# One stage for the four heads of a recurrent (mLSTM) layer, with the next head's products placed between the units of a head's recurrence

## The chip, the core and the metric

The kernel runs on one core of a Trainium2 chip. The metric is the device time of one execution in microseconds (us), median of the runs. A change of 0.3% is about 11 us here.

## The reference, cut to what matters

A four-layer network on 1024 tokens of width 1024. The change touches one mixer of it, the chunkwise mLSTM with 4 heads of width 192, chunks of 128 tokens, run once forward and once backward (`q` and `k` come from a convolved input, `k` with the factor 192 ** -0.5):

```
    def step(carry, inp):
        C, n, m = carry
        ...
        dexp = jnp.exp(d - m_t[..., None])
        iexp = jnp.exp(inter - m_t)
        s = jnp.einsum('bhtd,bhsd->bhts', qb, kb) * dexp
        num = jnp.einsum('bhts,bhse->bhte', s, vb) + iexp[..., None] * jnp.einsum('bhtd,bhde->bhte', qb, C)
        den = jnp.sum(s, axis=-1) + iexp * jnp.einsum('bhtd,bhd->bht', qb, n)
        h = num / jnp.maximum(jnp.abs(den), jnp.exp(-m_t))[..., None]
        ...
        C_new = cexp[..., None, None] * C + jnp.einsum('bhs,bhsd,bhse->bhde', wexp, kb, vb)
```

## The kernel before, in words

The program is a row of stages. Each stage is a block with its own semaphores: every engine runs its own instruction list, written out by hand in program order, and a barrier of all engines ends the stage. TensorE (PE) writes to eight PSUM banks, VectorE (DVE) and ScalarE (ACT) empty them. All matmuls of this part are in fp32; in the trace one such matmul is two MATMUL records.

`ml_layer` works the heads one after the other, with two stages for each, eight in all:

- `products` (L2025): PE makes qT and kT of the head (8 jobs of two matmuls of 512 columns, L2037), then its keys with the tokens on the partitions (8 jobs of two matmuls of 192 columns). The jobs go round all eight banks. DVE empties the even jobs (L158, L159), ACT the odd ones (L156).
- `recurrence` (L2296): PE spreads the gate sums over partitions (16 matmuls of 128 columns, L2325, into four banks, "spread") and makes q times k of each chunk (16 matmuls of 128 columns, L2332, "raw"). DVE zeroes the state (L2390) and adds a mask to each spread bank (L2394). ACT copies raw out of PSUM (L2365) and takes 16 exponentials (L2371), 8 for each direction. DVE multiplies exponentials and raw, one instruction for each direction (L2399), and that gives the weights of the two directions.
- Then come 16 units, in turn forward and backward. In a unit PE makes one matmul with the weights ("intra", L2345), two matmuls that update the state, from the keys scaled by ACT (L2351, kw L2378; not in the last two units), and two with the state ("inter", L2358). Each of these five has 193 columns. ACT scales inter into `carried` (L2385). DVE makes the new state (L2409), adds carried and intra to `num` (L2417), makes the denominator in three short instructions (L2421 to L2423) and writes the head's output (L2426 or L2430). PE may begin intra of unit u when num of unit u-2 is there.

After the fourth head comes the stage `head_norm` (L2435), which begins with DVE on `hs`.

## Time and profile before

| what | us |
|---|---|
| median of 3 runs (3794.08, 3789.55, 3781.88) | 3789.55 |
| the profiled execution, its own time | 3775.88 |
| its span in the profile | 3774.2 |
| PE busy in the span | 3372.5 (89%) |
| DVE busy | 1926.9 (51%) |
| ACT busy | 1375.9 (36%) |
| mean granted TensorE clock | 0.934 |

The profile is one execution. Its own time lies 13.67 us below the median of the three runs. A row of the timeline has the start and the duration, then engine, line, operation, output and inputs; in brackets stands how long the engine sat idle before it and who released it. A MATMUL's end is modelled. In a row of a list of stretches each engine has its busy us and its number of records. PEclk is the granted clock: 1.00 is 2.4 GHz, 0.50 is 1.2 GHz, and a figure between is a stretch that holds both.

### The profile page before, as it was taken

The numbers are of one execution on the slowest core, as the hardware profiler recorded it, in microseconds if no ns is written. First come the engines' busy times: TensorE is split into PE (matmuls) and PEld (weight loads), VectorE is DVE, ScalarE is ACT, GpSimd is POOL, SyncE is SP. The second block draws the span as 40 slices with busy tenths as digits, with TensorE's granted clock in tenths as the row PEclk, the third lists the DMA queues.
The fourth block names the chain that finished last, engine by engine and source line by source line (L and its number), as shares of the span: only waits on it lengthen the run. The fifth ranks groups of instructions, "written<-read, shape, count | busy, mean of one in ns | idle before, by whom it ended". The sixth has DMA issues, their size and how long they took to land. (4 is left out here: it accounts for less than half of the span.)

```text
span 3774.2 us, 51016 instructions
## 1 busy us (share of the span) xinstructions
PE 3372.5 (89%) x19671; PEld 2663.6 (71%) x19671; DVE 1926.9 (51%) x3394; ACT 1375.9 (36%) x2544; POOL 359.7 (10%) x295
## 2 busy tenths in 40 slices
PE   7999988799989978849789998799889999998899
PEld 6884466688857766647478887589755678885557
DVE  4526645657646735474647655623255442325554
ACT  2006641556642132233146555501254420114442
POOL 0100000223330000000023323100100000001000
PEclk9999999799999988869889999899889999988999
DMA  6517023678865200012258867511000221110003
GB/s 204 182 42 227 1 101 112 223 279 331 334 260 175 93 20 1 1 56 79 112 189 323 327 219 264 199 34 42 16 1 1 96 90 34 33 25 1 1 15 131
DMA packets 250408, 459.85 MB, mean 122 GB/s; under 512 B 45043, under 2 KB 118087, under 8 KB 249801
## 3 DMA queue, kind: packets, MB, share of 16 engines
q1 hardware_dynamic: 231753, 389.70, 29.3%
q0 software_dynamic: 18432, 67.12, 4.7%
q8 instruction: 148, 2.42, 0.3%
q14 instruction: 75, 0.61, 0.0%
HBM read 380.72 MB, written 73.33 MB: 120 GB/s over the span
## 5 line engine op out<-in xcount | busy, mean ns | idle before, releaser
L1727 PE MATMUL psum<-high_in,e_rowsT_high 128*128 128x256 f32 (+1 forms) x1080 | 330.1, 324 | 5.4 <-DVE e_rowsT_low L174 5.4
L1728 PE MATMUL psum<-high_in,e_rowsT_low 128*128 128x256 f32 (+1 forms) x1080 | 326.2, 320 | 0.0
L174 POOL TENSOR_TENSOR low_down<-w_down,high_out 128x1024 fp32r<-128x1024 f32 x64 | 192.6, 3026 | 326.0 <-ACT high_out L1801 326.0
L1727 PEld LDWEIGHTS psum<-high_in,e_rowsT_high 128*128 128x128 f32 x1080 | 206.6, 191 | 22.4 <-issue 6.1
L1728 PEld LDWEIGHTS psum<-high_in,e_rowsT_low 128*128 128x128 f32 x1080 | 206.9, 192 | 16.2
L3457 DVE TENSOR_REDUCE mla_low<-psum 128x1 f32<-128x256 f32 (+7 forms) x128 | 91.0, 753 | 151.6 <-PE psum L3323 151.6
L174 DVE TENSOR_TENSOR low_gate<-w_gate,high_in 128x1024 fp32r<-128x1024 f32 x128 | 147.9, 1218 | 0.1
L174 DVE TENSOR_TENSOR low_up<-w_up,high_in 128x1024 fp32r<-128x1024 f32 x128 | 148.0, 1218 | 0.0
L279 PE MATMUL psum<-ring_high,s_x_high 128*128 128x512 f32 (+3 forms) x768 | 135.4, 319 | 5.6 <-DVE ring_high L169 5.6
L283 PE MATMUL psum<-ring_low,s_x_high 128*128 128x512 f32 (+3 forms) x768 | 136.7, 321 | 2.9 <-DVE ring_low L174 2.9
L285 PE MATMUL psum<-ring_high,s_x_low 128*128 128x512 f32 (+3 forms) x768 | 134.8, 318 | 0.0
L1801 ACT ACTIVATE high_out<-w_down 128x1024 fp32r<-128x1024 f32 x128 | 124.8, 1050 | 23.8 <-DMA w_down<-in_exp_w_down 23.8
L1732 PE MATMUL psum<-low_up,e_rowsT_high 128*128 128x256 f32 x720 | 130.3, 283 | 0.0
L158 DVE COPY proj<-psum 128x512 f32<-128x512 f32 (+2 forms) x40 | 20.6, 514 | 212.8 <-PE psum L285 212.8
L279 PEld LDWEIGHTS psum<-ring_high,s_x_high 128*128 128x128 f32 x768 | 113.9, 191 | 16.5 <-issue 6.0
L156 ACT ACTIVATE proj<-psum 128x512 f32<-128x512 f32 (+2 forms) x40 | 18.3, 457 | 293.4 <-PE psum L285 293.4
L1801 ACT ACTIVATE high_in<-w_gate 128x1024 fp32r<-128x1024 f32 x128 | 124.8, 1058 | 0.0
L1801 ACT ACTIVATE high_in<-w_up 128x1024 fp32r<-128x1024 f32 x128 | 124.7, 1054 | 0.0
L283 PEld LDWEIGHTS psum<-ring_low,s_x_high 128*128 128x128 f32 x768 | 114.3, 192 | 14.5 <-DVE ring_low L174 4.0
L1856 POOL COPY e_index<-moe_ids 128x1 uint32 (+1 forms) x49 | 9.6, 195 | 1189.0 <-POOLq L84 563.8
L285 PEld LDWEIGHTS psum<-ring_high,s_x_low 128*128 128x128 f32 x768 | 113.9, 191 | 10.5
L156 ACT ACTIVATE mla_probsT<-psum 128x512 f32<-128x512 f32 (+2 forms) x96 | 52.2, 544 | 180.4 <-PE psum L3338 180.4
(592 smaller groups left out, 7945.9 us busy)
## 6 DMA issues: line engine op xcount, KB each, us to landing
w_gate<-in_exp_w_gate SPq DMA_DIRECT2D x32, 2048.0 KB, 10.3
w_up<-in_exp_w_up SPq DMA_DIRECT2D x32, 2048.0 KB, 15.3
w_down<-in_exp_w_down SPq DMA_DIRECT2D x32, 2048.0 KB, 21.9
ada<-in_ada_w SPq DMA_DIRECT2D x24, 1024.0 KB, 6.8
expert_rows<-e_out POOLq DMA_DIRECT2D x47, 512.0 KB, 7.0
expert_rows<-zero_row SPq DMA_DIRECT2D x33, 512.0 KB, 6.9
token_rows<-x SPq DMA_DIRECT2D x32, 512.0 KB, 2.6
x<-token_rows SPq DMA_DIRECT2D x24, 512.0 KB, 6.9
```

The lines of the kernel that those rows point to most:

```text
L156: return eng.activation(dst, src, ACT.Copy, scale=1.0 if scale is None else scale)
L158: return eng.tensor_copy(dst, src)
L174: return eng.tensor_tensor(low, whole, high, ALU.subtract)
L279: pe.matmul(dst, lhsT, rhs, start=(m == 0), stop=False)
L283: pe.matmul(dst, lhsT, rhs, start=False, stop=False)
L285: mm = pe.matmul(dst, lhsT, rhs, start=False, stop=(m == len(ops) - 1))
L1727: pe.matmul(dst, rows_high[:, k, :], w_high[:, k, cols], start=(k == 0), stop=False)
L1728: pe.matmul(dst, rows_low[:, k, :], w_high[:, k, cols], start=False, stop=False)
L1732: mm = pe.matmul(dst, rows_high[:, k, :], w_low[:, k, cols], start=False, stop=(k == KT - 1))
L1801: act.activation(high(e, j)[:, k:k + STEP[j], :], W[e % 2][j][:, k:k + STEP[j], :], ACT.Copy).then_inc(s["w_high_ready"], 1)
L1856: pool.tensor_copy(index[:, :], ids[:, bass.ds(i, 1)]).then_inc(s["index_ready"], 1)
L3457: dve.tensor_reduce(low[:, n, side:side + 1], scores_of(n, side), AX.X, ALU.min).then_inc(s["lows_ready"], 1)
```

## The change

`products` and `recurrence` go, and `heads` takes their place: one stage for all four heads. The work that prepares a head is cut into 18 items (`HeadItems`): 8 qk items (two matmuls of 512 columns each), 4 keys items (two token tiles, four matmuls of 192 columns, in one bank), 4 spread items (four of 128) and 2 raw items (eight of 128). Head 0's items run first, then its exponentials. In each unit of heads 0 to 2, PE makes one or two items of the next head behind its inter; units 14 and 15 have none. Items have two banks, 4 and 5, in turn, and an item waits until the item two before it is emptied. ACT now empties all qk, keys and raw items, behind `carried` of the same unit, and takes the next head's exponentials after units 12 and 13. DVE masks the next head's spreads after units 8 to 11 and makes its weights after units 14 and 15. qT, keys and decay have two buffers each, kT and raw one. The first two units of a head lose inter and carried (the state is zero there): the state and num are plain copies, and the zeroing of the state goes. The math is otherwise as before.

```diff
--- before.py
+++ after.py
@@ -1984,25 +1984,7 @@
-    for h in range(ML_HEADS):
...
-        products(nc, core, jobs)
-        recurrence(nc, core, h, qT, kT, keys, vals, table, hs)
+    heads(nc, core, xcT, wq, vals, table, hs)
...
+class HeadItems:
...
+        self.order = [("qk", j) for j in range(8)]
+        for m in range(4):
+            self.order += [("keys", m), ("spread", m)]
+        self.order += [("raw", 0), ("raw", 1)]
+        self.per_head = {"qk": 8, "keys": 4, "spread": 4, "raw": 2}
+        self.steps = [[("qk", u)] for u in range(8)] + [[("keys", m), ("spread", m)] for m in range(4)] + [[("raw", 0)], [("raw", 1)], [], []]
...
+    qT = [m.at("ml_qT", W + at * KB, [HF, 2, SEQ]) for at in (32, 96)]
+    kT = m.at("ml_kT", W + 40 * KB, [HF, 2, SEQ])
+    keys = [m.at("ml_k", at, [P, TILES, ML_DH]) for at in (AT_XT + 25 * KB, W + 112 * KB)]
+    decay = [m.at("r_decay", W + at * KB, [P, DIRS, TILES, P]) for at in (18, 104)]
...
+    def item_bank(kind, i):
+        return bank[4 + items.at(kind, i) % 2]
...
+            def prepare(H, kind, i):
+                earlier = items.two_earlier(kind, H, i)
+                if earlier:
+                    pe.wait_ge(emptied[earlier[0]], earlier[1])
+                dst = item_bank(kind, i)
+                if kind == "qk":
+                    a, n, cols, _ = qk_of(H, i)
+                    for j, f in pieces_of(H):
+                        mm = pe.matmul(dst[0:HF, :], wq.of(a, H, j)[:, n * HF:(n + 1) * HF], xcT[:, f, cols], start=(j == 0), stop=(j == 1))
+                    mm.then_inc(s["qk_ready"], 1)
...
+            for kind, i in items.order:
+                prepare(0, kind, i)
+            for h in range(ML_HEADS):
+                for u in range(U):
+                    n, d, chunk, j = unit(h, u)
+                    q = slice(chunk * P, (chunk + 1) * P)
+                    if u < DIRS:
+                        pe.wait_ge(s["probs_ready"], DIRS * h + u + 1)
+                    if U * h + u >= 2:
+                        pe.wait_ge(s["num_ready"], U * h + u - 1)
+                    pe.matmul(bank[u % 2][:, 0:DV], decay[h % 2][:, d, chunk, :], vals[:, chunk, h, :], start=True, stop=True).then_inc(s["intra_ready"], 1)
+                    if u < V:
+                        at = V * h + u
+                        pe.wait_ge(s["kw_ready"], at + 1)
+                        if at >= 2:
+                            pe.wait_ge(s["state_ready"], at - 1)
+                        for k in range(2):
+                            mm = pe.matmul(bank[6 + u % 2][0:HF, k * 256:k * 256 + DV], kw[:, at % 3, k * HF:(k + 1) * HF], vals[:, chunk, h, :],
+                                           start=True, stop=True)
+                        mm.then_inc(s["update_ready"], 1)
+                    if u >= DIRS:
+                        at = V * h + u - DIRS
+                        pe.wait_ge(s["state_ready"], at + 1)
+                        if at >= 2:
+                            pe.wait_ge(s["carried_ready"], at - 1)
+                        for k in range(2):
+                            mm = pe.matmul(bank[2 + u % 2][:, 0:DV], qT[h % 2][:, k, q], state[:, d, n % 2, k, :], start=(k == 0), stop=(k == 1))
+                        mm.then_inc(s["inter_ready"], 1)
+                    if h + 1 < ML_HEADS:
+                        for kind, i in items.steps[u]:
+                            prepare(h + 1, kind, i)
...
+                if kind == "raw":
+                    act.wait_ge(s["raw_ready"], items.count("raw", H, i))
+                    if H:
+                        act.wait_ge(s["probs_ready"], DIRS * H)
+                    act.activation(raw[:, 4 * i:4 * i + 4, :].rearrange("p c q -> p (c q)"), src, ACT.Copy).then_inc(s["raw_copied"], 1)
...
+            for kind, i in items.order:
+                copy_item(0, kind, i)
+            for d in range(DIRS):
+                exponents(0, d)
+            for h in range(ML_HEADS):
+                act.wait_ge(s["keys_copied"], 4 * h + 4)
+                for i in range(U + 1):
...
+                    if u >= DIRS:
+                        n, d, chunk, j = unit(h, u)
+                        act.wait_ge(s["inter_ready"], V * h + u - DIRS + 1)
+                        act.wait_ge(s["num_ready"], U * h + u - 1)
+                        act.activation(carried[:, u % 2, :], bank[2 + u % 2][:, 0:DV], ACT.Copy,
+                                       scale=E[:, IEXP * S + j:IEXP * S + j + 1]).then_inc(s["carried_ready"], 1)
+                    if u >= 0 and h + 1 < ML_HEADS:
+                        for kind, k in items.steps[u]:
+                            copy_item(h + 1, kind, k)
+                        if u in (12, 13):
+                            exponents(h + 1, u - 12)
...
+                        if u < DIRS:
+                            if h:
+                                dve.wait_ge(s["inter_ready"], V * h)
+                            dve.tensor_copy(state[:, d, 1, :, :], update).then_inc(s["state_ready"], 1)
...
+                    if u >= DIRS:
+                        dve.wait_ge(s["carried_ready"], V * h + u - DIRS + 1)
+                        dve.tensor_tensor(num[:, u % 2, :], carried[:, u % 2, :], bank[u % 2][:, 0:DV], ALU.add).then_inc(s["num_ready"], 1)
+                    else:
+                        dve.tensor_copy(num[:, u % 2, :], bank[u % 2][:, 0:DV]).then_inc(s["num_ready"], 1)
...
+                    if h + 1 < ML_HEADS:
+                        if 8 <= u < 12:
+                            mask(h + 1, u - 8)
+                        if u >= 14:
+                            weigh(h + 1, u - 14)
```

The order on PE around the end of head 0. Before (L2345 intra, L2351 update, L2358 inter, L2037 products, L2325 spread, L2332 raw; L81 is a stage's end):

```order
L2345 MATMUL psum<-ml_v_14671,r_decay_15158 128x193
L2358 MATMUL psum<-r_state_15160,ml_qT_15046 128x193 x2
L81 UNCONDITIONAL_BRANCH
L2030 UNCONDITIONAL_BRANCH
L2037 MATMUL psum<-ml_xcT_13226,ml_wqkv_14672 96x512 x16
L2037 MATMUL psum<-ml_wqkv_14672,ml_xcT_13226 128x192 x16
L81 UNCONDITIONAL_BRANCH
L2320 UNCONDITIONAL_BRANCH
L2325 MATMUL psum<-neg_uT_14692,consts_49 128x128 x16
L2332 MATMUL psum<-ml_qT_15755,ml_kT_15756 128x128 x16
L2345 MATMUL psum<-ml_v_14671,r_decay_15867 128x193
```

With the change, from unit 13 of head 0 to unit 0 of head 1 (L2358 intra, L2365 update, L2374 inter, L2345 raw, L2326 qk; decay 15051 is head 0's, 15052 head 1's):

```order
L2358 MATMUL psum<-ml_v_14671,r_decay_15051 128x193
L2365 MATMUL psum<-ml_v_14671,r_kw_15055 96x193 x2
L2374 MATMUL psum<-r_state_15054,ml_qT_15046 128x193 x2
L2345 MATMUL psum<-ml_qT_15047,ml_kT_15048 128x128 x8
L2358 MATMUL psum<-ml_v_14671,r_decay_15051 128x193
L2374 MATMUL psum<-r_state_15054,ml_qT_15046 128x193 x2
L2358 MATMUL psum<-ml_v_14671,r_decay_15051 128x193
L2374 MATMUL psum<-r_state_15054,ml_qT_15046 128x193 x2
L2358 MATMUL psum<-ml_v_14671,r_decay_15052 128x193
L2365 MATMUL psum<-ml_v_14671,r_kw_15055 96x193 x2
L2326 MATMUL psum<-ml_xcT_13226,ml_wqkv_14672 96x512 x2
```

The 64 matmuls that stood between two heads are spread over the units; six matmuls of 193 columns (units 14 and 15) now stand between the last raw item and the next head's first intra.

ACT at the same place with the change (L2418 kw, L2425 carried, L2396 raw copy, L2403 exponential), from the end of unit 12 on:

```order
L2425 ACTIVATE r_carried_15056<-psum,exps_14690 128x193
L2396 ACTIVATE r_raw_15053<-psum 128x512
L2403 ACTIVATE r_decay_15052<-r_decay_15052,a_14682 128x128 x8
L2425 ACTIVATE r_carried_15056<-psum,exps_14690 128x193
L2396 ACTIVATE r_raw_15053<-psum 128x512
L2403 ACTIVATE r_decay_15052<-r_decay_15052,a_14682 128x128 x8
L2425 ACTIVATE r_carried_15056<-psum,exps_14690 128x193 x2
L2418 ACTIVATE r_kw_15055<-ml_k_15050,exps_14690 128x192
```

Carried of units 13 and 14 now stands behind a raw copy and 8 exponentials each; before, `carried` alternated with kw alone. On DVE the next head's first weights stand between the last two units:

```order
L2489 SCALAR_TENSOR_TENSOR ml_hs_14673<-r_num_15057,r_den_15058,ml_hs_14673 128x192
L2444 TENSOR_TENSOR r_decay_15052<-r_decay_15052,r_raw_15053 128x1024
L2474 TENSOR_TENSOR r_num_15057<-r_carried_15056,psum 128x193
L2480 SCALAR_TENSOR_TENSOR r_den_15058<-r_num_15057 128x1
L2481 TENSOR_SCALAR r_den_15058<-r_den_15058,exps_14690 128x1
L2482 RECIPROCAL r_den_15058<-r_den_15058 128x1
L2489 SCALAR_TENSOR_TENSOR ml_hs_14673<-r_num_15057,r_den_15058,ml_hs_14673 128x192
L2444 TENSOR_TENSOR r_decay_15052<-r_decay_15052,r_raw_15053 128x1024
L2461 COPY r_state_15054<-psum 96x386
```

So the first weights (the first L2444) wait for the output of unit 14 of the head before, and the second for that of unit 15.

## Rows read from the trace of the kernel before

**Rows 1.** The page's first line, and the stretch of the four heads (engines' busy us, clock)

```profile
span 3774.2 us, 51016 instructions
...
1363.00:1641.00 278.00, 238.24 (x1120) 182.89 (x1120) 147.49 (x436) 84.45 (x225) 0.00 (x0) 0.89 0.00 1
```

**Rows 2.** Timeline, head 0 from its first product to its first unit

```profile
1363.87 15.64 PE L2037 MATMUL psum<-ml_xcT,ml_wqkv 128*96 128x512 f32 x32 [2.94 <-PEq L84]
...
1379.35 5.36 PE L2037 MATMUL psum<-ml_wqkv,ml_xcT 128*128 128x192 f32 x32
...
1385.79 3.81 PE L2325 MATMUL psum<-neg_uT,consts 64*128 64x128 f32 x32 [1.08 <-PEq L84]
...
1389.53 3.84 PE L2332 MATMUL psum<-ml_qT,ml_kT 96*128 96x128 f32 x32
...
1393.40 0.60 ACT L2365 ACTIVATE r_raw<-psum 128x512 f32<-128x512 f32 x1 [1.19 <-PE psum L2332]
1393.90 4.77 ACT L2371 ACTIVATE r_decay<-r_decay,a 128x128 f32<-128x128 f32 x16
1396.44 1.22 DVE L2399 TENSOR_TENSOR r_decay<-r_decay,r_raw 128x1024 f32<-128x1024 f32 x1 [6.11 <-ACT r_decay L2371]
...
1397.81 0.98 PE L2345 MATMUL psum<-ml_v,r_decay 128*128 128x193 f32 x2 [4.44 <-DVE r_decay L2399]
...
1402.52 0.36 DVE L2417 TENSOR_TENSOR r_num<-r_carried,psum 128x193 f32<-128x193 f32 x1 [1.12 <-ACT r_carried L2385]
```

**Rows 3.** Timeline, end of head 0 and start of head 1's products

```profile
1427.85 0.35 DVE L2417 TENSOR_TENSOR r_num<-r_carried,psum 128x193 f32<-128x193 f32 x1
...
1429.20 0.35 DVE L2417 TENSOR_TENSOR r_num<-r_carried,psum 128x193 f32<-128x193 f32 x1
...
1431.46 16.59 PE L2037 MATMUL psum<-ml_xcT,ml_wqkv 128*96 128x512 f32 x32 [3.32 <-PEq L84]
```

**Rows 4.** Timeline, first unit of head 3 and last instruction of the fourth recurrence

```profile
1606.57 0.98 PE L2345 MATMUL psum<-ml_v,r_decay 128*128 128x193 f32 x2 [4.44 <-DVE r_decay L2399]
...
1640.23 0.42 DVE L2430 SCALAR_TENSOR_TENSOR ml_hs<-r_num,r_den,ml_hs 128x192 f32<-128x192 f32 x1
```

**Rows 5.** Timeline, copies of every second 512-column product in head 0

```profile
1370.97 0.69 DVE L158 COPY ml_qT<-psum 96x512 f32<-96x512 f32 x1 [3.90 <-PE psum L2037]
...
1374.40 0.69 DVE L159 TENSOR_SCALAR ml_kT<-psum 96x512 f32<-96x512 f32 x1 [2.75 <-PE psum L2037]
```

**Rows 6.** Timeline, intra of two early units and num of two late units of head 0

```profile
1403.85 0.49 PE L2345 MATMUL psum<-ml_v,r_decay 128*128 128x193 f32 x2
...
1405.48 0.49 PE L2345 MATMUL psum<-ml_v,r_decay 128*128 128x193 f32 x2
...
1418.96 0.35 DVE L2417 TENSOR_TENSOR r_num<-r_carried,psum 128x193 f32<-128x193 f32 x1
...
1420.84 0.34 DVE L2417 TENSOR_TENSOR r_num<-r_carried,psum 128x193 f32<-128x193 f32 x1
```

**Rows 7.** Groups by line in the heads' stretch: busy us, mean ns, idle before

```profile
L2409 DVE SCALAR_TENSOR_TENSOR r_state<-r_state,exps,psum 96x386 f32<-96x386 f32 x56 | 34.0, 607 | 3.8 <-PE psum L2351 3.8
L2385 ACT ACTIVATE r_carried<-psum,exps 128x193 f32<-128x193 f32 x64 | 27.1, 423 | 74.5 <-PE psum L2358 74.5
L2378 ACT ACTIVATE r_kw<-ml_k,exps 128x192 f32<-128x192 f32 x56 | 24.5, 444 | 0.0
...
L156 ACT ACTIVATE ml_kT<-psum 96x512 f32<-96x512 f32 x8 | 4.7, 593 | 22.7 <-PE psum L2037 22.7
```

**Rows 8.** Stretches of 2 us of PE's clock around first units (heads 0 and 3)

```profile
1396.00:1398.00 2.00, 0.19 (x1) 0.22 (x2) 1.22 (x1) 2.00 (x9) 0.00 (x0) 0.50 0.00 0
...
1402.00:1404.00 2.00, 2.00 (x11) 1.93 (x11) 1.35 (x6) 0.75 (x2) 0.00 (x0) 0.83 0.00 0
1404.00:1406.00 2.00, 2.00 (x15) 2.00 (x14) 1.68 (x7) 1.08 (x3) 0.00 (x0) 1.00 0.00 0
...
1614.00:1616.00 2.00, 2.00 (x13) 1.98 (x13) 1.37 (x6) 0.88 (x3) 0.00 (x0) 0.93 0.00 0
```

More of the change, by code:

```diff
@@ L2311, in recurrence, with unit @@
     S = STREAMS
-    def unit(u):
+    k_scale = ML_DH ** -0.5
+    items = HeadItems()
+    def unit(h, u):
         n, d = divmod(u, DIRS)
@@ L2316, in unit, with qk_of @@
         return n, d, chunk, stream(d, chunk, h)
-    with stage(nc, "state_zeroed", "spread_ready", "raw_ready", "raw_copied", "masked", "decayed", "probs_ready", "kw_ready", "intra_ready",
-               "update_ready", "inter_ready", "carried_ready", "num_ready", "den_steps", "state_ready", "h_ready") as (block, s):
+    def item_bank(kind, i):
+        return bank[4 + items.at(kind, i) % 2]
+    def qk_of(H, j):
+        a, n, half = j // 4, j // 2 % 2, j % 2
+        return a, n, slice(half * BANK, (half + 1) * BANK), (kT if a else qT[H % 2])
@@ L2320, in _ @@
+    with stage(nc, "qk_ready", "qk_copied", "keys_ready", "keys_copied", "spread_ready", "masked", "raw_ready", "raw_copied", "decayed", "probs_ready",
+               "kw_ready", "intra_ready", "update_ready", "inter_ready", "carried_ready", "num_ready", "den_steps", "state_ready", "h_ready") as (block, s):
+        emptied = {"qk": s["qk_copied"], "keys": s["keys_copied"], "spread": s["masked"], "raw": s["raw_copied"]}
         @block.tensor
         def _(pe):
-            for d in range(DIRS):
-                for chunk in range(TILES):
-                    j = stream(d, chunk, h)
-                    mm = pe.matmul(bank[2 * d + chunk // 4][:, (chunk % 4) * P:(chunk % 4 + 1) * P],
-                                   c["ident"][0:S, j:j + 1].to_broadcast([S, P]), table.nuT[:, :], start=True, stop=True)
-                    if chunk % 4 == 3:
-                        mm.then_inc(s["spread_ready"], 1)
@@ L2388, in _ @@
         @block.vector
         def _(dve):
-            dve.memset(state[:, :, :, :, :], 0.0).then_inc(s["state_zeroed"], 1)
-            for g in range(4):
-                dve.wait_ge(s["spread_ready"], g + 1)
-                mask = c["neg_future"] if g < 2 else c["neg_past"]
-                dve.tensor_tensor(decay[:, g // 2, 4 * (g % 2):4 * (g % 2) + 4, :], bank[g][:, :].rearrange("p (c q) -> p c q", c=4),
-                                  mask.unsqueeze(1).to_broadcast([P, 4, P]), ALU.add).then_inc(s["masked"], 1)
@@ L2396, in _, with mask, weigh @@
-            dve.wait_ge(s["raw_copied"], 2)
+            def mask(H, i):
+                dve.wait_ge(s["spread_ready"], items.count("spread", H, i))
+                hidden = c["neg_future"] if i < 2 else c["neg_past"]
+                dve.tensor_tensor(decay[H % 2][:, i // 2, 4 * (i % 2):4 * (i % 2) + 4, :], item_bank("spread", i).rearrange("p (c q) -> p c q", c=4),
+                                  hidden.unsqueeze(1).to_broadcast([P, 4, P]), ALU.add).then_inc(s["masked"], 1)
+            def weigh(H, d):
+                dve.wait_ge(s["raw_copied"], 2 * H + 2)
+                dve.wait_ge(s["decayed"], DIRS * H + d + 1)
+                dve.tensor_tensor(decay[H % 2][:, d, :, :], decay[H % 2][:, d, :, :], raw[:, :, :], ALU.mult).then_inc(s["probs_ready"], 1)
```

211 lines of the change are left out of this document (87 added, 124 removed).

## The prediction

> **What bounds the kernel now.** I first read the list of stretches for the part that the change touches, since a share of the whole span says nothing about it. The four heads take from 1363.87 us (first product of head 0) to 1640.65 us (end of the last output, 1640.23 + 0.42): 276.8 us [rows 2, 4]. That is 7% of the span of 3774.2 us [rows 1]. In the stretch PE is busy 238.2 us of 278, DVE 147.5, ACT 84.5, and the mean granted clock is 0.89 [rows 1]. So PE bounds it, yet some 40 us of it have no matmul, and some matmuls run at the low clock. No transfer matters here: the last column is 1 GB/s.
>
> Then I read the timeline of one head to see where PE idles. [Rows 2] show head 0: products, an idle 1.08 us at a stage's end, spread, raw, and then 4.44 us in which PE waits for the raw copy, 8 exponentials and the first weights. [Rows 3] show the end of a head: PE idles 3.32 us before the next head's first product, while DVE finishes the last two units. One head costs 1431.46 - 1363.87 = 67.6 us [rows 2, 3].
>
> Last, I read what sets the pace of a unit. Early units follow each other by 1405.48 - 1403.85 = 1.63 us: five matmuls of 193 columns back to back, 0.327 us each, so PE is the bound. Late units follow by 1420.84 - 1418.96 = 1.88 us, and there DVE is the bound [rows 6]. Sixteen units and their edges take far longer than PE's part of them.
>
> **PE's own work, at the high clock.** A product of 512 columns costs (1374.40 - 1370.97) / 4 = 0.857 us [rows 5]. The 16 of a head cost 13.7 us. The keys cost 5.36 less about 0.16 for the modelled end of the last matmul, 5.2 us, and spread and raw 3.8 us each [rows 2]. That makes 26.5 us of items for each head. A head's units hold 16 + 28 + 32 = 76 matmuls before and 72 with the change (two units lose their two inters), 72 x 0.327 = 23.5 us. So a head is 50.0 us of PE work against 51.3 before. The move hides no PE work, since items and units are both PE's. What can go is PE's idle time, its low clock, and DVE's 1.88 us pace, because a unit with an item needs 3.1 to 3.9 us of PE (1.63 plus 1.71 for a qk item; plus 1.3 and 0.95 for keys and spread; plus 1.9 for a raw item).
>
> **Term A, head 0 until its first unit.** Before: 1397.81 - 1363.87 = 33.9 us [rows 2]. The work is the same and in nearly the same order. Two banks in place of eight do not hold it: a qk item is 1.71 us of PE, and its copy on ACT is 0.59 us [rows 7], done long before the item after the next. The stage's end goes, 1.08 us. The memset of the state goes too, at no gain: it ran beside the spreads. A = 32.9 us.
>
> **Term B, three heads with items between the units.** In each I take 50.0 us of PE, and then look for waits.
> - Within the units: intra of unit u needs num of unit u-2. A whole unit of over 3 us lies between, and DVE needs under 1.9 us for a unit [rows 6]. kw of unit u+1 stands on ACT behind the item copy of unit u-1; it ends about 1.25 us after that item (0.2 to start, then 0.59 and 0.44 [rows 7]), and PE wants it one unit later, after 3.6 us. That leaves 2.4 us. Both cost nothing as long as this cover holds; a miss by x costs x in each of 42 units. ACT also takes DVE's share of the copies, some 4 us a head; beside its 84.5 us of busy time [rows 1] that leaves it far from full.
> - At the end of a head there is a chain, and this is the step I trust least. After the last raw item ACT starts its copy at 0.25 us and the exponentials 0.5 us later. Eight of them at (4.77 - 0.39) / 15 = 0.29 us take 2.35 us [rows 2]. Only then comes carried of unit 14, which stands behind them: 3.1 us, and with 0.42 and a handover its num starts at 3.6 us. DVE finishes that unit in 1429.20 - 1427.85 = 1.35 us [rows 3], makes the first weights in 1.22 us plus 0.15 until PE starts [rows 2], and PE begins the next head at 6.3 us. In that time PE has six matmuls, 1.96 us. It idles 4.3 us at each of the three ends. The second weights come 2.6 us later (unit 15 and 1.22), beside 0.98 us of matmuls and a qk item of 1.71 us: no further wait in heads 1 and 2.
> - Clock: after the 4.44 us of idle time the clock was at the low level at both first units shown. It came back about 4.9 us after the first intra in head 0 (0.83 in 1402 to 1404), and 7.7 us after it in head 3 (0.93 in 1614 to 1616) [rows 2, 4, 8]. At half speed that costs 2.4 to 3.9 us of PE work. An idle time of 4.3 us should do the same; some of it hides behind waits, and I take 2.7 us a head. Update of unit 0 in head 0 also waits some 0.5 us for kw.
>
> B = 3 x (50.0 + 4.3 + 2.7) + 0.5 = 171.5 us.
>
> **Term C, head 3 without items.** Before: 1640.65 - 1606.57 = 34.1 us [rows 4]. DVE's pace stays. What goes is the start: the first num came 1402.52 - 1397.81 = 4.7 us after the first intra [rows 2], behind update, inter and carried at the low clock. Now it needs neither inter nor carried, only the second weights (2.4 us) and a copy of the state like L2409's 0.61 us [rows 7], so 3.1 us. Two units without the last add save up to 1 us more. Bounds: 30.8 us (nothing at the low clock) and 34.1 us (no gain). I take 31.5 us.
>
> **The sum.** 32.9 + 171.5 + 31.5 = 235.9 us against 276.8 us: 40.9 us less, rounded to 41. What follows is `head_norm`, which starts on the end of the outputs, and all later stages only move forward. The profiled execution would go from 3775.88 us to about 3735 us. It lies 13.67 us under the median of the runs shown, so I put the gain on the median: 3789.55 - 41 = 3748.5 us.
>
> **A rule weighed against the rows.** In the steady units PE has short pauses for num and goes round PSUM banks, and the clock stayed at 1.00 there (1404 to 1406) [rows 8]; the sum keeps the high clock in all units but those after a long idle time. The Trainium skill (TensorE: Matmul & The Clock Gate, section "A second HAM failure mode: psum-queue depth-cycling") says that a kernel whose PE idles briefly between groups of matmuls, going from bank to bank, can see its clock swing between the two levels. By that rule this change, which puts two banks in place of eight and a handover behind each item, would pay at the low clock what it wins in idle time. The trace does not bear it out for pauses of this size.
>
> **Rivals.**
> 1. *The covers are thinner than I think.* If in-order ACT and DVE hold PE by 0.3 us in each of the 42 units that make items, 12.6 us go, and a gain of 28 us is left: 3761 us. For it: carried, kw, copy and exponentials now share one queue. Against it: the margin of 2.4 us above. Chance 0.10.
> 2. *The head's end is cheaper.* If the clock does not fall in 4.3 us of idle time (8 us) and head 3 starts as fast as it can, the gain is 50 us: 3739.5 us. Against it: it fell both times in [rows 8]. Chance 0.10.
> 3. *The clock falls inside the units.* This is the way to slower. The place is the unit loop of heads 0 to 2, 150 us of PE work. Each us of work at the low level costs one more us. The gain of 41 us is used up once 41 of the 150 us (27%) run at 1.2 GHz. With half of it there, 75 us are added: 34 us slower, 3823.5 us. Against it are the steady units of [rows 8]. Chance 0.03.
> 4. *The move brings nothing.* PE already bounds the stretch, and if its idle time only comes back elsewhere (each unit waits about 0.9 us longer, 38 us over 42 units), the time stays within 5 us of 3789.5 us. Chance 0.02.
>
> **How the numbers follow.** Forecast 0.75, with 3748.5 us as the likeliest. The terms' bounds are 2.4 to 3.9 us of clock for each head and 30.8 to 34.1 us for head 3; with a median's own scatter (the three runs span 12 us) they give 3740 to 3757 us. The range takes in rivals 1 and 2 with some of that scatter: 3736 to 3766 us. No change means within 0.3%, 11 us, about what a measurement of this kernel can tell. Faster 0.95 (forecast, 1 and 2), same 0.02 (4), slower 0.03 (3).
>
> **What would show it.** In the profile after: first product of head 0 to last output about 236 us; PE idle of about 4.3 us before intra of units 0 of heads 1 to 3, released by DVE's weights; the distance between these units about 57 us; no PE idle over 0.3 us in units 2 to 13; low clock only at head 0's products and after the long idle times; ACT's exponentials directly ahead of carried of units 13 and 14. It is wrong if PE waits in the middle units for a copy, a mask or kw, if the idle at a head's end is over 6 us, or if the clock there is under 0.9 as a mean.

## The result, and the profile after

The change takes 3748.14 us (median of 4 runs, 3736.74 to 3751.73) beside 3787.55 us before: ratio 0.9893, interval 0.9871 to 0.9916, so 1.1% faster. The same kernel built and run once more gave 3742.76 beside 3784.43 us, ratio 0.9893, interval 0.9877 to 0.9910. In its profile the stretch of the heads is 238.9 us and PE waits 4.07 us at each of the three heads' ends, as in the first profile, which is shown below.

The first profiled execution took 3748.63 us; that of before took 3775.88 us. Its span is 27.3 us shorter, but the heads' stretch is 38.1 us shorter: the first product already came at 1374.02 us and not at 1363.87 [rows 2], after stages whose code is the same. Such a scatter of 10 us ahead of the stretch is also seen between the experiments below, so they are read by the stretch (first product of head 0 to the end of the last output), and the times only confirm it.

The page's first line and the stretch, as [rows 1]; then stretches of 2 us at head 0's start, around the first unit of head 1 and in middle units, as [rows 8] (us; busy us of PE, PEld, DVE, ACT, POOL; granted clock; DMA share; GB/s):

```profile
span 3746.9 us, 50783 instructions
...
1374.00:1613.00 239.00, 218.50 (x1088) 170.48 (x1088) 131.48 (x400) 92.13 (x232) 0.00 (x0) 0.94 0.00 1
...
1376.00:1378.00 2.00, 2.00 (x4) 0.75 (x3) 0.00 (x0) 0.59 (x1) 0.00 (x0) 0.50 0.00 0
...
1434.00:1436.00 2.00, 2.00 (x8) 0.96 (x7) 1.28 (x5) 0.42 (x1) 0.00 (x0) 1.00 0.00 0
1444.00:1446.00 2.00, 2.00 (x14) 1.88 (x13) 1.13 (x3) 0.14 (x1) 0.00 (x0) 1.00 0.03 8
...
1464.00:1466.00 2.00, 0.12 (x1) 0.12 (x2) 1.93 (x5) 0.10 (x1) 0.00 (x0) 1.00 0.00 0
1466.00:1468.00 2.00, 2.00 (x7) 1.37 (x8) 1.86 (x6) 0.00 (x0) 0.00 (x0) 0.69 0.00 0
1468.00:1470.00 2.00, 2.00 (x4) 0.86 (x3) 1.86 (x7) 0.00 (x0) 0.00 (x0) 0.50 0.00 0
1470.00:1472.00 2.00, 2.00 (x9) 1.35 (x9) 0.50 (x2) 0.94 (x2) 0.00 (x0) 0.96 0.00 0
```

In the middle units PE is full at the high clock (1.00). The clock is low at head 0's start, around head 0's first unit (from 1404 to 1413 us), and around and behind the idle time at a head's end.

The timeline of the change: first product, first unit of head 0, the end of head 0 with the start of head 1, and the last output (as [rows 2 to 4]):

```profile
1374.02 0.64 PE L2326 MATMUL psum<-ml_xcT,ml_wqkv 128*96 128x512 f32 x1 [2.95 <-PEq L84]
...
1407.91 1.01 PE L2358 MATMUL psum<-ml_v,r_decay 128*128 128x193 f32 x2 [4.35 <-DVE r_decay L2444]
...
1460.37 2.43 ACT L2403 ACTIVATE r_decay<-r_decay,a 128x128 f32<-128x128 f32 x8
...
1460.99 0.82 PE L2374 MATMUL psum<-r_state,ml_qT 96*128 96x193 f32 x4
1462.70 0.71 ACT L2425 ACTIVATE r_carried<-psum,exps 128x193 f32<-128x193 f32 x2
1463.24 0.36 DVE L2474 TENSOR_TENSOR r_num<-r_carried,psum 128x193 f32<-128x193 f32 x1 [1.97 <-ACT r_carried L2425]
...
1464.60 1.22 DVE L2444 TENSOR_TENSOR r_decay<-r_decay,r_raw 128x1024 f32<-128x1024 f32 x1
...
1465.88 0.59 PE L2358 MATMUL psum<-ml_v,r_decay 128*128 128x193 f32 x2 [4.07 <-DVE r_decay L2444]
...
1612.32 0.42 DVE L2489 SCALAR_TENSOR_TENSOR ml_hs<-r_num,r_den,ml_hs 128x192 f32<-128x192 f32 x1
```

This is the chain that the prediction wrote down: the second batch of exponentials, carried of unit 14 behind it, its num, then the first weights, and PE idle for 4.07 us until they are there. The other two ends have the same 4.07 us. The first units of the heads are at 1407.91, 1465.88, 1523.14 and 1581.19 us.

| part | forecast, us | measured, us |
|---|---|---|
| head 0 until its first unit | 32.9 | 33.9 |
| heads 0 to 2, first unit to first unit | 57.2 each, 171.5 | 57.97, 57.26, 58.05: 173.3 |
| head 3 | 31.5 | 31.6 |
| stretch | 235.9 | 238.7 (before 276.8) |

Where the 38.1 us came from. Time of the stretch without a matmul went from 276.8 - 238.2 = 38.6 to 238.7 - 218.5 = 20.2 us: 18.4 us. Over all stretches of 2 us, PE's busy time at the low clock went from about 46.6 to about 20.6 us; the low level is half of the high one, so the work would have taken half of that time at the high clock, and the difference is worth 13.0 us. Sixteen matmuls fewer (two units of four heads, two each) at 0.327 us are 5.2 us. That is 36.6; 1.5 us are not assigned. Two terms of opposite sign lie in that rest. The late units of a head before followed each other by 1.78 to 1.88 us and not by 1.63, and most of that shows as no idle time, because a matmul's modelled end covers it: about 1.7 us a head, 5 us in the three heads whose units now have items. And the alternating keys and spread items cost PE 1.0 us in head 0 and 1.2 us in each of the others (experiment 4), 4.8 us. Both are estimates from rows of the timelines. They nearly cancel, so most of the 1.5 us stays open.

### The profile page after: what moved, and what is told of

The parts are those of the page before. It is cut to its first block and busy times, and to the rows that moved or that the text cites. A ratio compares the mean times of both kernels' runs of the same rounds, so it can differ in the third digit from the quotient of the medians.

```text
span 3746.9 us, 50783 instructions
## 1 busy us (share of the span) xinstructions
PE 3355.3 (90%) x19639; PEld 2654.9 (71%) x19639; DVE 1911.1 (51%) x3358; ACT 1383.2 (37%) x2552; POOL 359.4 (10%) x295
```

## The experiments

Each is read by where its first units stand and by PE's idle times. "Distance" is from the first unit of a head to that of the next.

**1. Is it the placing between the units?** The stage and its lighter first units stay, but all items of the next head, its masks, exponentials and weights come behind unit 15:

```diff
-        self.steps = [[("qk", u)] for u in range(8)] + [[("keys", m), ("spread", m)] for m in range(4)] + [[("raw", 0)], [("raw", 1)], [], []]
+        self.steps = [[] for _ in range(15)] + [self.order]
```

> One stage for all heads as in the change, but nothing is interleaved: all 18 items, masks, exponentials and weights of the next head come behind unit 15. Theory (most of the gain comes from the barriers, with their idle time and low clock, and from the lighter first units, not from placing items between units): a head takes about 59.5 us (before: 68.4; less 3.3 and 1.1 us of idle time at the stages' ends, less about 2.9 us of low clock behind the first, less about 1.6 us of the first two units), so the stretch of the heads is about 245 us and the whole 32 us faster than before. Rival (the interleaving makes the gain): a head stays within 3 us of the 68.4 us of before, the stretch is 268 us or more and the whole at most 9 us faster than before.

It took 3757.65 us, ratio 0.9920, interval 0.9897 to 0.9942. The stretch is 248.9 us, distances 60.79, 61.07 and 61.25:

```profile
1474.98 1.01 PE L2358 MATMUL psum<-ml_v,r_decay 128*128 128x193 f32 x2 [4.34 <-DVE r_decay L2445]
...
1502.82 0.59 PE L2358 MATMUL psum<-ml_v,r_decay 128*128 128x193 f32 x2 [0.63 <-DVE r_num L2475]
```

(Timeline of this kernel, first and last unit of head 1.) The idle time at the start of a head is 4.34 us, nearly the 4.44 us of before, and the last units follow each other by 1.88 us, DVE's pace, as in [rows 6]; 0.63 us of idle time shows ahead of the last one. So of the 38 us the placing brings some 10 (248.9 - 238.7), and the single stage with its lighter first units 28 (276.8 - 248.9). The two times alone would not show this split (0.9920 and 0.9893, with intervals that overlap); the stretches do. 

Where the 28 us come from can be followed: PE's idle time in the stretch is 23.8 us against 38.6 (14.8 less), its work at the low clock 22.7 us against 46.6 (12.0 us of time), and the sixteen matmuls are 5.2 us; the alternating keys and spread items take back about 4 us (experiment 4), which the expected 245 us lacked. What the placing adds is mainly that the items cover DVE's pace in the late units (about 5 us), 3.6 us less idle time and 1.0 us less low clock. So most of the gain lies in the stage ends, in the low clock behind them, and in the work left out.

**2. Does DVE's order set the idle time at the head's end?** The first weights go behind unit 13 on DVE, not behind unit 14:

```diff
-                        if u >= 14:
-                            weigh(h + 1, u - 14)
+                        if u in (13, 15):
+                            weigh(h + 1, (u - 13) // 2)
```

> Only VectorE's first weights of the next head move: behind unit 13 in place of unit 14. Theory (the idle time at a head's end is the chain exponentials, carried and num of unit 14, its output, weights): PE's wait before a head's first intra falls from 4.07 us to about 1.9 us, now released by num of unit 14, and one of about 0.9 us for the second weights appears behind the first item; the clock falls less or not at all, so a head is 1.5 to 4 us shorter and the stretch of the heads 4 to 12 us shorter than with the change. Rival (PE waits for the exponentials on ScalarE, wherever the weights stand): the wait stays at 4 us and the stretch at 239 us.

It took 3733.93 us, ratio 0.9855, interval 0.9831 to 0.9879; stretch 231.9 us, distances 55.94, 54.24 and 55.09. The timeline at the end of head 1:

```profile
1512.19 1.22 DVE L2444 TENSOR_TENSOR r_decay<-r_decay,r_raw 128x1024 f32<-128x1024 f32 x1
1514.25 0.36 DVE L2474 TENSOR_TENSOR r_num<-r_carried,psum 128x193 f32<-128x193 f32 x1 [0.84 <-ACT r_carried L2425]
...
1514.75 0.90 PE L2358 MATMUL psum<-ml_v,r_decay 128*128 128x193 f32 x2 [1.94 <-DVE r_num L2474]
```

The weights now lie in DVE's wait for carried of unit 14. PE waits 1.94 us, and for num: what is left is ScalarE's batch of exponentials. The wait for the second weights also came, 0.56 us in head 1 and 2.28 us in head 3, where no item stands between the two. The clock stayed at 1.00 behind the 1.93 us at the end of head 0 and fell to 0.50 behind the 1.94 us at the end of head 1, so the third distance (55.09), which begins with that low clock, is longer than the second (54.24).

**3. What is the idle time worth, and its clock?** Twelve matmuls of 192 columns are added behind unit 15 of heads 0 to 2, in PE's idle time. Nothing reads their results.

```diff
+                if h + 1 < ML_HEADS:
+                    pe.wait_ge(s["raw_copied"], 2 * h + 3)
+                    for _ in range(12):
+                        pe.matmul(item_bank("raw", 0)[:, 0:ML_DH], xcT[:, 0, 0:P], wq.of(1, 0, 0), start=True, stop=True)
```

> Twelve added matmuls of 192 columns (3.9 us, their result is not used) behind unit 15 of heads 0 to 2, in PE's idle time of 4.07 us. Theory (the idle time costs twice, by itself and by the low clock after it): the distance from head to head stays at 55 us (50.0 of work, 4.1 of filled idle time, about 1.3 of slower keys and spread items) instead of 57.3 to 58.0, since the clock stays high: the stretch is 7 to 9 us shorter than with the change although PE does 12 us more. Rival (the low clock behind the idle time is hidden by waits): the stretch stays at 239 us or grows.

It took 3741.06 us, ratio 0.9875, interval 0.9852 to 0.9898; stretch 233.2 us, 5.5 under the change's and not 7 to 9. The end of head 0 in its timeline, and the clock behind it:

```profile
1459.78 0.59 PE L2358 MATMUL psum<-ml_v,r_decay 128*128 128x193 f32 x2 [0.17 <-DVE r_decay L2448]
```

```profile
1460.00:1462.00 2.00, 2.00 (x9) 1.35 (x9) 1.87 (x5) 0.00 (x0) 0.00 (x0) 1.00 0.00 0
```

Instructions were added and the stretch got shorter: the clock stays at 1.00. (The times of the two kernels, 0.9875 and 0.9893, have intervals that overlap.) Distances two and three are 55.57 us each, against 57.26 and 58.05 with the change. The filled time is as long as the idle one, so the difference, 1.7 and 2.5 us, 2.1 us as a mean, is the clock alone. The prediction had taken 2.7 us. Head 3 is 0.9 us shorter as well (it waits 1.25 us for its second weights). So 5.1 of the 5.5 us stand behind the three filled idle times; the first distance has none before it, and there a shorter start of head 0 (32.2 us, see Term A) and a longer first distance (59.28 against 57.97) nearly cancel. It also says what a head costs PE without idle time and at the high clock: 55.57 - 12 x 0.327 - 0.17 = 51.5 us, where the prediction had 50.0.

**4. Where do 1.5 us of PE work come from?** The middle units with a keys and a spread item take (1452.72 - 1435.95) / 4 = 4.19 us, where the sum of their matmuls is 3.88. The timeline of the change, units 9 and 10, with PE's weight loads:

```profile
1443.20 0.96 PEld L2337 LDWEIGHTS psum<-neg_uT,consts 64*128 64x128 f32 x8 [0.23 <-issue]
1443.20 1.16 PE L2337 MATMUL psum<-neg_uT,consts 64*128 64x128 f32 x8
...
1444.28 0.30 PEld L2358 LDWEIGHTS psum<-ml_v,r_decay 128*128 128x128 f32 x2
1444.28 0.59 PE L2358 MATMUL psum<-ml_v,r_decay 128*128 128x193 f32 x2
1444.55 0.65 PEld L2365 LDWEIGHTS psum<-ml_v,r_kw 128*96 128x96 f32 x4
1444.71 0.82 PE L2365 MATMUL psum<-ml_v,r_kw 128*96 128x193 f32 x4
```

The loads of the update (L2365) start 0.16 us ahead of its matmuls. Those of the spread, which have 64 rows, and those of intra right behind them start with the matmuls. If this costs time at each change between 64 rows and 128, fewer changes must be faster. Two keys items and then two spread items share a unit:

```diff
-        for m in range(4):
-            self.order += [("keys", m), ("spread", m)]
+        self.order += [("keys", m) for m in range(4)] + [("spread", m) for m in range(4)]
```

(The steps and the masks of the units follow it.)

> The order of the items alone changes: two keys items in each of units 8 and 9, two spread items in each of units 10 and 11, in place of one of each in four units. Seen in the trace after: units 8 to 11 follow each other by 4.22 us, where the matmuls' sum is 3.88; behind a spread item (64 rows of the array in use) and ahead of it the weight load doesn't run ahead of the matmul. Theory (each change between 64 and 128 rows costs 0.1 to 0.15 us): the four units together take 16.9 us in the change and 16.2 here, 0.7 us less in each head, 2 us over the stretch. Rival (each item's start and hand-over costs that, whatever its rows): 16.9 us, no change.

Units 8 to 11 took 1446.34 - 1430.34 = 16.00 us against 16.77: 0.77 us a head less, as expected. Head 0, which has its items in a row, took 32.88 us from its first product to its first unit against 33.89, both with a low clock at the start: 1.0 us less. The one run took 3743.61 us. The distances did not get shorter (57.82, 57.60 and 57.81, in sum 173.2 as with the change) and the stretch is 238.3 us: PE was busy for some 26 us at the low clock, not 20.6, and the 3 us or a little less that this costs are nearly what the grouping saves in four heads (3.3 us).

**5. Is the lighter start of a head worth something by itself?** The kernel before, with only its first two units made lighter (no inter and carried, plain copies, no zeroing of the state), in eight stages as before:

```diff
-                if i >= 1:
+                if i >= 3:
...
-            dve.memset(state[:, :, :, :, :], 0.0).then_inc(s["state_zeroed"], 1)
```

> The kernel before with one part of the change alone: the first two units of a head without inter and carried, plain copies for state and num, no zeroing of the state; eight stages and their barriers stay. Theory: four matmuls fewer a head are 1.3 us of TensorE, and the first num comes earlier; together 1.3 to 2.5 us a head, so the stretch of the heads is 267 to 272 us against 276.8. Rival (this part carries much of the 38 us): over 4 us a head, the stretch 260 us or less.

It took 3776.51 us beside 3779.15 us, ratio 0.9989, interval 0.9976 to 1.0002: no difference; stretch 277.0 us. The expectation failed. The four recurrences' units did get shorter, from 33.65, 33.51, 33.47 and 34.07 to 32.17, 32.57, 31.98 and 31.58 us (first unit to the next head's first product, or to the last output). But the parts between (first product to first unit) grew from 33.94, 34.89, 34.83 and 38.41 to 33.94, 38.72, 37.15 and 38.86 us. 36 us from about the first product of heads 1, 2 and 3 (before: 1431.46, 1499.86 and 1568.16), before and then in this kernel:

```profile
1431.00:1467.00 36.00, 30.02 (x130) 19.01 (x130) 9.27 (x14) 9.35 (x26) 0.00 (x0) 0.88 0.00 0
1499.00:1535.00 36.00, 29.62 (x129) 18.79 (x130) 9.32 (x15) 9.01 (x25) 0.00 (x0) 0.88 0.00 1
1567.00:1603.00 36.00, 32.51 (x128) 21.55 (x128) 8.39 (x14) 5.13 (x12) 0.00 (x0) 0.82 0.00 1
```

```profile
1432.27:1468.27 36.00, 33.20 (x128) 22.90 (x128) 6.95 (x12) 5.99 (x15) 0.00 (x0) 0.81 0.00 0
1503.56:1539.56 36.00, 31.63 (x128) 21.24 (x128) 7.18 (x13) 7.56 (x20) 0.00 (x0) 0.84 0.00 1
1572.28:1608.28 36.00, 32.97 (x128) 22.91 (x128) 6.95 (x12) 5.44 (x13) 0.00 (x0) 0.81 0.00 1
```

The same products and spreads ran at a mean clock of 0.81 to 0.84, not 0.82 to 0.88. Of the 6.6 us that these parts grew, low clock makes 5.7 (57.9 us of work at the low clock in the whole stretch, 46.6 before). It does not stand behind the 3.3 us of idle time, where there is less of it than before. It stands in the spread and raw products, behind the short idle time of 1.07 us at the end of `products`. Head 1 in the kernel before, its spread and 2 us of it, and then the same in this one:

```profile
1454.34 3.81 PE L2325 MATMUL psum<-neg_uT,consts 64*128 64x128 f32 x32 [1.08 <-PEq L84]
...
1458.00:1460.00 2.00, 2.00 (x19) 1.93 (x18) 0.69 (x1) 0.00 (x0) 0.00 (x0) 1.00 0.00 0
```

```profile
1454.12 5.40 PE L2325 MATMUL psum<-neg_uT,consts 64*128 64x128 f32 x32 [1.07 <-PEq L84]
...
1458.00:1460.00 2.00, 2.00 (x10) 1.78 (x9) 0.99 (x2) 0.00 (x0) 0.00 (x0) 0.50 0.00 0
```

At this place 10.0, 6.8 and 10.1 us of work ran at the low clock in heads 1, 2 and 3 here; before, only head 3 had such a spell (6.8 us, behind 1.46 us of idle time), which is why its part took 38.41 us. So a short stage end is followed by a low clock in some heads and not in others, and why is open. The 276.8 us of before hold one such spell, worth 3.4 us; whether every execution of that kernel has it is not shown, since only one was profiled. The time says only that the whole kernel did not get faster by more than 0.24%; the 6.4 us in the units are read from one profile.

**6. Can the idle time at the head's end go?** Everything is placed two units earlier: two qk items in units 0 and 1, exponentials behind units 10 and 11, weights behind units 11 and 14. The second kernel also has the items of experiment 4.

```diff
-                        if u in (12, 13):
-                            exponents(h + 1, u - 12)
+                        if u in (10, 11):
+                            exponents(h + 1, u - 10)
...
-                        if u >= 14:
-                            weigh(h + 1, u - 14)
+                        if u in (11, 14):
+                            weigh(h + 1, (u - 11) // 3)
```

> The change with the next head's items two units earlier (two qk items in each of units 0 and 1, raw items in units 10 and 11), exponentials behind carried of units 10 and 11, first weights behind unit 11 on VectorE and second behind unit 14; no instruction more or fewer. Theory (the wait at a head's end is only the chain behind the last raw item, and the units after it can cover it): the 4.07 us fall to under 1.5 us in pieces and the clock stays high, so a head is 4 to 6 us shorter: 51.5 to 53.5 us, and the stretch of the heads 221 to 227 us against 238.7. Rival (the chain only moves with the items, because carried of the units behind the exponentials is late there too): a head stays above 55.5 us, the stretch above 232 us.

> As e5, and the keys and spread items grouped as in e4. Theory: the two gains add, since one is idle time and the other is TensorE's own time: 0.7 us a head less than e5, the stretch 2 to 3 us shorter than e5's and the whole 15 to 19 us faster than the change. Rival: the wait grows by what the items shrink, and the stretch is e5's.

The first took 3726.93 us, ratio 0.9860, interval 0.9840 to 0.9880; stretch 227.8 us, distance 54.08. The second took 3728.17 us, ratio 0.9855, interval 0.9836 to 0.9875; stretch 227.2 us, distance 53.31, so again 0.77 us a head by the grouping. The stretches differ by 0.65 us and not by the 2 to 3 expected, since the second kernel has 8.5 us of work at the low clock, all in head 0, against 3.0 in the first: 2.7 us. The first kernel also gains 1.7 us on the change by the clock at head 0's start (see Term A), which the new order did not bring. The long idle time is gone, and so is the low clock behind it (4.4 us of the first kernel's stretch are at the low level, 27.4 us of the change's). A wait of 1.44 us is left at each head's end, at an update, for its scaled keys, and 0.95 and 0.51 us at the start of head 3, which has no items.

**7. What is that wait?** I first took it for the next head's scaled keys behind the last carried, and moved those ahead:

```diff
-                    if i < V:
+                    if i < V and (h == 0 or i >= 2):
                         weigh_keys(h, i)
+                    if i in (V, V + 1) and h + 1 < ML_HEADS:
+                        weigh_keys(h + 1, i - V)
```

> As e6, and ScalarE scales the keys of the next head's first two units (kw 0 and 1) ahead of carried of units 13 and 14 in place of behind carried of unit 15. In e6 TensorE waits 1.44 us before a head's first update for this kw, which stands behind carried of unit 15. Theory: that wait goes at the three ends, a head is 51.9 us in place of 53.3, the stretch 222 to 224 us in place of 227.2, and the whole about 4 us faster than e6. Rival (behind that wait is another, the next num or the second weights, that ends as late): the stretch stays above 226 us.

It took 3734.37 us, ratio 0.9865, interval 0.9849 to 0.9882; stretch 226.4 us, distance 52.98, and the wait was still there. Its timeline, end of head 1, ScalarE and then PE:

```profile
1511.91 2.44 ACT L2402 ACTIVATE r_decay<-r_decay,a 128x128 f32<-128x128 f32 x8
1514.25 0.45 ACT L2416 ACTIVATE r_kw<-ml_k,exps 128x192 f32<-128x192 f32 x1
```

```profile
1512.82 0.49 PE L2357 MATMUL psum<-ml_v,r_decay 128*128 128x193 f32 x2
1514.75 0.90 PE L2364 MATMUL psum<-ml_v,r_kw 128*96 128x193 f32 x4 [1.44 <-ACT r_kw L2416]
```

I had read the wrong unit. The update that waits is that of unit 12, and its keys stand behind the eight exponentials that follow unit 10. So these keys went ahead of the exponentials:

```diff
                         if u in (10, 11):
+                            weigh_keys(h, u + 2)
                             exponents(h + 1, u - 10)
```

> e8_keys_scaled_ahead with one more ordering: on ScalarE the keys of units 12 and 13 of each head that has a next one are scaled directly ahead of the two batches of eight exponentials, not behind them; nothing else is changed. Corrected reading of the 1.44 us wait that e8 left (at 1461.77, 1514.75 and 1567.73): it is the update of unit 12 waiting for its scaled keys, which stand on ScalarE behind the eight exponentials that follow unit 10 (2.44 us). If that is the cause, the wait is gone at all three heads, the distance of two heads falls from 52.98 to 51.5 to 51.9 us and the stretch from 226.4 to 221.5 to 223.5 us. Rival: ScalarE itself is full there (eight exponentials 2.44, scaled keys 0.45, carried 0.4 us in a unit of 3.3 us), so that the carried copy of unit 11 is late in its place: a wait of 0.8 us or more of the product of unit 13 for the vector engine's numerator, distance 52.5 to 53.2, stretch 225 to 227.

It took 3726.63 us, ratio 0.9859, interval 0.9843 to 0.9875, but the stretch is 227.6 us: the wait came that the rival had named. Its timeline at the end of head 0, then the clock at the end of head 1:

```profile
1447.37 2.44 ACT L2402 ACTIVATE r_decay<-r_decay,a 128x128 f32<-128x128 f32 x8
...
1449.71 0.41 ACT L2430 ACTIVATE r_carried<-psum,exps 128x193 f32<-128x193 f32 x1
...
1450.66 0.59 PE L2357 MATMUL psum<-ml_v,r_decay 128*128 128x193 f32 x2 [0.93 <-DVE r_num L2480]
...
1452.55 0.59 PE L2357 MATMUL psum<-ml_v,r_decay 128*128 128x193 f32 x2 [0.63 <-DVE r_num L2480]
```

```profile
1506.00:1508.00 2.00, 2.00 (x8) 2.00 (x7) 1.83 (x8) 0.30 (x1) 0.00 (x0) 0.50 0.00 0
```

The wait moved from the keys to carried, which now is late behind the same batch: 0.93 + 0.63 us in place of 1.44. Unit 13 of head 1 follows that of head 0 by 52.98 us, as in the kernel before this one. That the stretch is even 1.2 us longer is the clock: it fell to 0.50 behind the two waits in heads 1 and 2 (not in head 0), and 14.5 us of work are at the low clock against 8.4, worth 3.0 us. Without that the stretch would be the shorter of the two, so it is the waits and the 52.98 us that carry this reading.

**8. Is it the length of the batch?** Starting from the kernel with the keys scaled ahead (not from the last one), the exponentials come in fours, behind units 9 to 12:

```diff
-                        if u in (10, 11):
-                            exponents(h + 1, u - 10)
+                        if 9 <= u < 13:
+                            exponents(h + 1, u - 9)
```

> e8_keys_scaled_ahead with the next head's sixteen exponentials cut into four batches of four, behind units 9, 10, 11 and 12, in place of two batches of eight behind units 10 and 11; nothing else is changed, and the order of the scaled keys is e8's. e9 showed that no order of ScalarE's instructions around a batch of eight (2.44 us) is free: scaled keys behind it cost 1.44 us, the carried copy behind it 0.93 + 0.63 us. A batch of four is 1.24 us; with scaled keys 0.45, carried 0.41 and an item's copy 0.58 that is 2.7 us of ScalarE in a unit of 3.4 us. If the length of a batch is the cause, no wait over 0.5 us is left in units 9 to 15 of heads 0 to 2, the distance of two heads is 51.4 to 52.0 us (e8: 52.98) and the stretch 221.5 to 224 us (e8: 226.4). Rival: the time is ScalarE's sum, or the next link (the second batch's end, weights 0 at unit 11) is late: a new wait of 1 us or more at units 11 to 15 or at the next head's first unit, distance 52.6 or more.

It took 3729.61 us (3722.03 to 3741.13) beside 3782.65 us, ratio 0.9855, interval 0.9829 to 0.9881. The stretch is 1587.70 - 1367.06 = 220.6 us (its last row is below), the second and third distances are 51.76 and 51.77, and the only waits at a head's end are short; 1.27 and 0.51 us are left in the first units of head 3:

```profile
1446.73 1.27 ACT L2402 ACTIVATE r_decay<-r_decay,a 128x128 f32<-128x128 f32 x4
...
1448.40 0.90 PE L2364 MATMUL psum<-ml_v,r_kw 128*96 128x193 f32 x4 [0.23 <-ACT r_kw L2417]
...
1452.54 0.57 PE L2357 MATMUL psum<-ml_v,r_decay 128*128 128x193 f32 x2 [0.20 <-DVE r_num L2480]
...
1587.28 0.42 DVE L2495 SCALAR_TENSOR_TENSOR ml_hs<-r_num,r_den,ml_hs 128x192 f32<-128x192 f32 x1
```

```profile
1367.00:1589.00 222.00, 209.30 (x1088) 165.42 (x1088) 129.55 (x402) 92.66 (x233) 0.00 (x0) 0.98 0.00 1
```

PE is busy 209.3 of the 220.6 us, and the mean clock of the window is 0.98; the largest idle time left is the 4.35 us ahead of head 0's first unit. By the stretch this is the best version, 56.1 us under before and 18.1 under the change. Not all of that is the order: of the 5.8 us against the kernel that it starts from, 1.7 are head 0's start, where the clock did not fall in this execution (31.17 us against 32.87), and that put the stretch under the expected 221.5 us. The distances, 51.8 us against 53.0, are what the shorter batches bring. By the times, the kernels of experiments 2, 6, 7 and 8 all lie between 0.9855 and 0.9865, and their intervals overlap: their order among themselves is known from the traces alone. Experiment 6 has two such kernels and experiment 7 two, so these are six; all lie under the change's 0.9893. Their intervals still touch its own, but in every trace the stretch is 7 to 18 us shorter.

## Why the prediction was right

- **What bounds the stretch** (PE's work, its idle time and its clock): right. PE's idle time and low clock make 31.4 of the 38.1 us, and experiment 8 took most of the rest: from 20.6 to 4.1 us of work at the low clock, and from 20.2 to 11.3 us of idle time.
- **Term A**, 32.9 us, measured 33.9 us. The stage's end went as forecast. The missing 1.0 us is a cost that the term had put at nothing ("the work is the same and in nearly the same order"): keys and spread items now alternate, and where they are grouped the part takes 32.88 us (experiment 4). The clock at the start is a second matter. It is low there in before (33.94 us), in the change, and in experiments 1, 2 and 4; in experiment 3 and in the first kernel of 6 it stayed at 1.00, and the same head 0 took 32.19 us. In the grouped order the two values are 32.87 and, in experiment 8, 31.17. So such a start costs 1.7 us in some executions and nothing in others. Two microseconds of it, in experiment 4 and in experiment 3:

```profile
1370.00:1372.00 2.00, 2.00 (x3) 0.62 (x3) 0.00 (x0) 0.29 (x1) 0.00 (x0) 0.50 0.00 0
```

```profile
1370.00:1372.00 2.00, 2.00 (x6) 0.81 (x5) 0.00 (x0) 0.60 (x2) 0.00 (x0) 1.00 0.00 0
```

- **Term B**, 57.2 us a head, measured 57.8. The chain at the head's end was right link by link: 4.3 forecast, 4.07 measured, and experiment 2 moved it by moving one link. The 0.5 us for the update of unit 0 in head 0 came as 0.33. The clock was sized at 2.7 and is 2.1 (experiment 3). "50.0 us of PE work" was too low: 51.5, and 1.2 of these 1.5 us are in the four units with a keys and a spread item (16.77 against 4 x 3.88), since the loads of the spread's 64 rows and of intra behind them are not hidden. [Rows 2] hold 32 such matmuls in one row, with no change between shapes in it; I had priced the item but not its neighbours. 51.5 + 4.07 + 2.1 = 57.7. That the term came out within 0.6 us is in part luck: 1.5 us too little work and 0.8 us too much idle time and clock.
- **"Both cost nothing"** for num and kw in the middle units: right, no idle time over 0.3 us in units 2 to 13. Rival 1 (thinner covers, 12.6 us) did not come.
- **Term C**, 31.5 us, measured 31.6. Right as a sum. Experiment 5 made this part of the change alone: head 3's units took 31.58 us there, from 34.07. It also shows that such a gain can be lost to the clock elsewhere.
- **Rival 2** (the clock doesn't fall): wrong, it went to 0.50 behind each of the three idle times. **Rival 3** (it falls inside the units): it stayed at 1.00 in all of them. By the Trainium skill (TensorE: Matmul & The Clock Gate, section "A second HAM failure mode: psum-queue depth-cycling") short pauses from bank to bank could have made it swing; in this trace the profile shows no idle time of PE over 0.3 us between the matmuls of the middle units, so the two banks left no pause in which to test that.
- **The gain on the median**: 41 us forecast, ratio 0.9893 makes 40.5 us (32 to 49). The profile's stretch gives 38.1 us, of a forecast 40.9.
- What the prediction did not ask: how much of the gain the interleaving brings. It is about a quarter; one stage in place of eight is the larger part.

## What to carry to other kernels

Where two pieces of work share the bounding engine, placing one inside the other hides none of that engine's work, only the pace of its helpers (about 5 us here); count what the seams cost (stage ends, drained pipelines, the clock behind them), as one merged stage without any interleaving already gave 28 of 38 us here. Then look at the in-order helpers: a batch of 2.44 us on ScalarE delays whatever stands behind it, changing the order only chooses the victim, and cutting the batch in two left waits of 0.2 us. And name the unit that waits before mending a wait; the same label stood for two different units here.

## What was unexpected of the hardware

- A change between stationary tiles of 64 and of 128 rows keeps the weight load from running ahead of the matmuls. In the grouped order a head has two spells of 64 rows and not four, so four changes fewer, and 0.77 us less in experiments 4 and 6: 0.19 us for a change. In head 0 it is one spell in place of four, six changes fewer, and 1.0 us less: 0.17 us for a change. Changes between 128 rows and the 96 of inter show no such thing: its loads start ahead of its matmuls (at 1445.21 and at 1445.37 us, in unit 10 of the change).
- A gain of 6.4 us in the units of the kernel before was given back as low clock in the products that follow (experiment 5), at the same lengths of idle time. Between such versions the clock must be read before a mechanism is called false.
- The length of an idle time did not settle whether the clock fell. Behind 1.44 us it stayed at 1.00 at all nine heads' ends (experiment 6 and the first kernel of 7). Behind 0.93 and 0.63 us it fell in two heads of three (experiment 7), behind 1.93 us it stayed and behind 1.94 us it fell (experiment 2), and behind 1.07 or 1.08 us it fell in two heads of three (experiment 5) and in none of three before. The change's own two executions agree within 0.2 us, but other kernels here differ by 1.7 to 3 us through the clock alone, so a difference of that size between two profiles is to be read together with the clock.
- Filling a PE idle time of 4 us with useless matmuls at three heads' ends made the stretch 5.5 us shorter (experiment 3), 5.1 of them behind the filled idle times, where the clock stayed up.
